# Layer norms of a two-block network: statistics gathered while the products before run, the norm's end on columns of 128 tokens, and constant products on TensorE around it

## The reference, abridged

```python
def layer_norm(x, g, b):
    mu = jnp.mean(x, -1); var = jnp.mean(jnp.square(x - mu), -1)
    return (x - mu) * lax.rsqrt(var + LN_EPS) * g + b
...
    for i in range(DEPTH):            # 2 layers: gated delta net, then short conv mixer
        h = layer_norm(ALPHA * h + mix, ...)                       # norms 0 and 2
        h = layer_norm(ALPHA * h + conv_ffn(h, ...), ...)          # norms 1 and 3
...
    x = x + 0.5 * g1 * swiglu(modulate(rms_norm(x, ...)), ...)     # norm 4
    x = x + g2 * mixer(modulate(rms_norm(x, ...)))                 # norm 5
    x = x + 0.5 * g3 * swiglu(modulate(rms_norm(x, ...)), ...)     # norm 6
    return rms_norm(x, final_norm)                                 # norm 7
```

## Time and profile before

| | us |
|---|---|
| median of 3 runs | 1393.05 (1392.62 to 1393.16) |
| the profiled execution's own time | 1394.26 |
| its span in the trace | 1392.6 |
| TensorE busy | 1309.7 (94%) |
| VectorE busy | 989.1 (71%) |
| ScalarE busy | 792.6 (57%) |

### The profile page before, as it was taken

One profiled execution on the slowest core, in us unless ns is written; L12 is line 12 of the kernel. 1 busy time (PEld: TensorE's weight loads), 2 busy tenths in 40 slices (PEclk: granted clock), 3 DMA queues, 4 the chain that ended last, 5 costly groups with the idle time before them and its releaser, 6 DMA issues.

```text
span 1392.6 us, 28808 instructions
## 1 busy us (share of the span) xinstructions
PE 1309.7 (94%) x10370; PEld 1280.7 (92%) x10370; DVE 989.1 (71%) x1727; ACT 792.6 (57%) x1165; POOL 45.2 (3%) x83
## 2 busy tenths in 40 slices
PE   6997999899999999999999889999899999999997
PEld 5996999789999889889999789999799988999996
DVE  7777653879897789779894577774556666777744
ACT  5868233477773354477773467763455554777632
POOL 0001000000001101000100000000000000000000
PEclk9989999999999999999999989999999999999998
DMA  6431002438788768648785435565445334465651
GB/s 234 148 110 60 1 32 76 167 121 275 273 305 292 257 200 282 227 140 289 275 296 183 130 92 188 186 210 184 155 137 167 122 107 136 150 198 181 217 179 42
DMA packets 65339, 244.44 MB, mean 176 GB/s; under 512 B 7264, under 2 KB 9600, under 8 KB 65280
## 3 DMA queue, kind: packets, MB, share of 16 engines
q1 hardware_dynamic: 54624, 204.70, 43.9%
q0 software_dynamic: 10656, 38.93, 8.5%
HBM read 242.56 MB, written 1.05 MB: 175 GB/s over the span
## 4 chain that ended last, share of the span: by engine, by line
PE 86%; DVE 7%; ACT 5%; issue 2%; DMA 0%; DVEq 0%; ACTq 0%; SPq 0%
PE ps L1375 23%; PE ps L1376 23%; PE ps L1377 23%; PE ps L1389 2%; PE ps L1507 2%; PE ps L1517 2%; DVE wlo L319 2%; PE ps L1390 1%; PE ps L1620 1%; DVE tb L863 1%; PE ps L1395 1%; ACT whi L312 1%; PE ps L1666 1%; PE ps L1455 1%; PE ps L1668 1%
## 5 line engine op out<-in xcount | busy, mean ns | idle before, releaser
L1375 PE MATMUL ps<-hhi,whi 128*128 128x258 f32 (+4 forms) x2064 | 591.6, 287 | 7.3 <-DVE ab L1243 2.7
L1376 PE MATMUL ps<-hlo,whi 128*128 128x258 f32 (+4 forms) x2064 | 587.7, 285 | 0.0
L1377 PE MATMUL ps<-hhi,wlo 128*128 128x258 f32 (+4 forms) x2064 | 586.8, 284 | 0.0
L312 ACT ACTIVATE whi<-raw 128x1024 fp32r<-128x1024 f32 (+1 forms) x360 | 399.9, 1112 | 284.5 <-PE ps L1377 261.6
L319 DVE TENSOR_TENSOR wlo<-raw,whi 128x1024 fp32r<-128x1024 f32 (+1 forms) x360 | 462.2, 1292 | 109.6 <-ACT whi L312 108.4
L1375 PEld LDWEIGHTS ps<-hhi,whi 128*128 128x128 f32 x2064 | 393.6, 191 | 8.6 <-issue 6.1
L1376 PEld LDWEIGHTS ps<-hlo,whi 128*128 128x128 f32 x2064 | 394.0, 191 | 0.5 <-issue 0.2
L1377 PEld LDWEIGHTS ps<-hhi,wlo 128*128 128x128 f32 x2064 | 394.4, 191 | 0.0
L1375 PE MATMUL ps<-ahi,whi 128*128 128x256 f32 (+2 forms) x768 | 216.0, 281 | 1.4 <-DVE alo L1156 1.4
L1376 PE MATMUL ps<-alo,whi 128*128 128x256 f32 (+2 forms) x768 | 216.3, 282 | 0.0
L1377 PE MATMUL ps<-ahi,wlo 128*128 128x256 f32 (+2 forms) x768 | 215.8, 281 | 0.0
(11 more groups left out here) (339 smaller groups left out, 1468.8 us busy)
## 6 DMA issues: line engine op xcount, KB each, us to landing
raw<-in_w_up SPq DMA_DIRECT2D x176, 512.0 KB, 3.5
raw<-in_w_down SPq DMA_DIRECT2D x64, 704.0 KB, 4.3
ring<-in_ada_w POOLq DMA_DIRECT2D x72, 512.0 KB, 4.5
raw<-in_w_mix SPq DMA_DIRECT2D x48, 512.0 KB, 3.4
raw<-in_w_a_in SPq DMA_DIRECT2D x32, 512.0 KB, 3.5
raw<-in_w_b_cx SPq DMA_DIRECT2D x16, 512.0 KB, 4.4
raw<-in_w_a_out SPq DMA_DIRECT2D x8, 512.0 KB, 3.5
raw<-in_w_b_gate SPq DMA_DIRECT2D x8, 512.0 KB, 4.4
```

What stands on the lines that cost most here:

```text
L312: nc.scalar.activation(whi[:, s, 0:blocks * P], raw[:, s, 0:blocks * P], ACT.Copy).then_inc(hi_split, 1)
L1375: nc.tensor.matmul(out, whi[:, s, w], rhi(k0 + k), start=first and k == 0, stop=False)
L1376: nc.tensor.matmul(out, whi[:, s, w], rlo(k0 + k), start=False, stop=False)
L1377: ins = nc.tensor.matmul(out, wlo[:, s, w], rhi(k0 + k), start=False, stop=last and k == blocks - 1)
```

## The change

- **Layer norms 0 to 3.** A provisional mean (`shift`) is taken from the first two tiles by one PE product in the middle of the phase (`shift_mm`). DVE subtracts it from the tiles already there, and from the residual before later tiles are added (`centre_residual`). ACT squares each tile during the phase (`act_before_ln`), DVE sums the squares (`square_up`). When the last tile comes, only its own sum and square are missing.
- **Columns.** PE multiplies data (as weights) by one column of `C_MEAN` (`columns`), so that the sums of 128 tokens stand as one column of 128 partitions. Variance, guess and Newton step run on 3 columns (2 where there are 256 tokens). `row` spreads a column back over all partitions by a transpose of a broadcast column. What is left of the mean (`rest`) is subtracted tile by tile (`take_rest`), for tiles 0 to 3 ahead of the gain products, for 4 to 7 between them.
- **Norms 5 and 7** get the same end; seven tiles' squares are reduced on PE before the last half unit (`seven_squares_mm`).
- **Constant products.** `keep_busy` issues 3 and then 4 fp32 products of constants (10 after norm 3, none in norm 7) around the last `row`.
- **first_step** runs tile by tile over three slots at once (two for `x`, `rms0`, `rms2`).
- The split of the last slot before the norm (`meanwhile`) moves from the middle of `dve_norm` to its end. The PE programs of `down0`, `down1`, `b_out` and `a_out` are written out instead of looped. ACT's 1/sqrt table is loaded ahead of the last tile, and the Silu table right after the guess, and the reloads inside the `up` loops are gone. POOL's first loads for `ada_w` wait until `a_out` is done. `spread` uses banks 1, 4, 5, 6, 0 so that bank 2 is free for the third slot. `down_squares` and `act_down_squares` are reordered around the last tile in the same manner.

```diff
-SUMS_AT = {i: i * KT for i in range(8)}
+SUMS_AT = {0: 0, 1: 7, 2: 14, 3: 21, 4: 28, 5: 36, 6: 43, 7: 51}
+LN_AHEAD = 4
+IDLE_PRODUCTS = {0: (3, 4), 1: (3, 4), 2: (3, 4), 3: (3, 10), 5: (3, 4), 7: (0, 0)}
+SC_REST, SC_REST2, SC_VAR, SC_GUESS, SC_TMP, SC_RSTD = range(320, 344, 4)
+RAW_TILES = {"a_out": 3, "down0": 2, "b_out": 3, "down1": 2}
+SHIFT_TILES = 2
...
+        def groups_of(n):
+return 2 if n == SEQ else 3
+        def group(n, j):
+o = j * P if (j + 1) * P <= n else n - P
+return slice(o, o + P)
...
+pool.wait_ge(tiles_read, SLOTS + PH["up0"].first)
...
+def act_before_ln(i, name, n):
+    phase = PH[name]
+    per = 2 if phase.blocks == SLOT_BLOCKS else 1
+    t0, k, after = phase.first // SLOTS, phase.units // SLOTS, BLOCKS_AFTER[name]
+    if name != "a_out":
+        mine(nc.scalar.activation(small[:, 314:315], eps_of(LN_EPS), ACT.Abs_reciprocal_sqrt))
+    def square(m):
+        act.wait_ge(xc_ready, i * KT + m + 1)
+        if m >= 2:
+            act.wait_ge(sq_sum, i * (KT - 1) + max(2, m - 1))
+        nc.scalar.activation(ab[:, m % 2, 0:n], xb[:, m, 0:n], ACT.Square).then_inc(sq_ready, 1)
+    done = 0
+    for u in range(phase.units):
+        if u == phase.units - 1:
+            square(KT - 1)
+        split_hi(act, t0 + u // SLOTS + 1, u % SLOTS, phase.blocks if u // SLOTS < k - 1 else after)
+        tiles = (u + 1) // per
+        if name == "a_out" and u == SLOTS:
+            act.wait_ge(ld_c, 16)
+            nc.scalar.activation(cb[:], cb[:], ACT.Silu).then_inc(c_ready, 1)
+            act.wait_ge(eps_ready, 1)
+            mine(nc.scalar.activation(small[:, 314:315], eps_of(LN_EPS), ACT.Abs_reciprocal_sqrt))
+        if u % per == per - 1 and tiles > RAW_TILES[name] and tiles < KT:
+            while done < tiles:
+                square(done)
+                done += 1
...
+    g = groups_of(n)
+    if i < 4:
+        act.wait_ge(v_ready, i + 1)
+        nc.scalar.activation(sc(SC_GUESS, g), sc(SC_VAR, g), ACT.Abs_reciprocal_sqrt).then_inc(guess_ready, 1)
+        if i in (0, 2):
+            mine(nc.scalar.activation(small[:, 312:313], eps_of(eps), ACT.Silu))
+    else:
+        act.wait_ge(var_mm, i + 1)
+        nc.scalar.activation(sc(SC_GUESS, g), ps[5][:, 0:g], ACT.Abs_reciprocal_sqrt, bias=eps_of(eps)).then_inc(guess_ready, 1)
...
+    mine(nc.scalar.activation(small[:, 312:313], eps_of(RMS_EPS), ACT.Silu))
...
+def dve_residual(norm, name, n, off):
...
+    t0, k, after, raw_tiles = phase.first // SLOTS, phase.units // SLOTS, BLOCKS_AFTER[name], RAW_TILES[name]
+    shift, squares = tb[:, 0, 0:n], sb[:, 0, 0:n]
+    x_of = lambda m: xb[:, m, 0:n]
+    h_of = lambda m: hf[:, m, off:off + n]
+    def lo_of(u):
+        split_lo(dve, t0 + u // SLOTS + 1, u % SLOTS, phase.blocks if u // SLOTS < k - 1 else after)
+    def sum_up(m):
+        if m == 0:
+            return
+        dve.wait_ge(tiles_read, SLOTS + phase.first + (m + 1) * per)
+        if m > 1:
+            dve.wait_ge(sum_ready, SUMS_AT[norm] + m)
+        nc.vector.tensor_tensor(sums[:, 0:n], x_of(0) if m == 1 else sums[:, 0:n], x_of(m), ALU.add).then_inc(sum_ready, 2 if m == 1 else 1)
+    def square_up(m):
+        dve.wait_ge(sq_ready, norm * KT + m + 1)
+        if m > 1:
+            dve.wait_ge(sq_sum, norm * (KT - 1) + m)
+        if m:
+            nc.vector.tensor_tensor(squares, ab[:, 0, 0:n] if m == 1 else squares, ab[:, m % 2, 0:n], ALU.add).then_inc(sq_sum, 2 if m == 1 else 1)
+    def centre_residual(m):
+        step(nc.vector.scalar_tensor_tensor(h_of(m), h_of(m), ALPHA, shift, ALU.mult, ALU.subtract))
+    squared = 0
+    for m in range(KT):
+        u = (m + 1) * per - 1
+        if m == KT - 1 and per == 2:
+            lo_of(u - 1)
+        dve.wait_ge(unit_done, phase.first + u + 1)
+        bank = ps[(u - per + 1) % SLOTS][:, 0:n]
+        if m < raw_tiles:
+            nc.vector.scalar_tensor_tensor(x_of(m), h_of(m), ALPHA, bank, ALU.mult, ALU.add).then_inc(tiles_read, per)
+            if m < SHIFT_TILES:
+                sum_up(m)
+        else:
+            nc.vector.tensor_tensor(x_of(m), h_of(m), bank, ALU.add).then_inc(xc_ready, 1)
+            if m == KT - 1:
+                break
+            nc.vector.memset(small[:, 310:311], 0.0).then_inc(tiles_read, per)
+            sum_up(m)
+            centre_residual(m + 1)
+        for j in range(u - per + 1, u + 1):
+            lo_of(j)
+            if per == 2 and j == u - 1:
+                while m > raw_tiles and squared < m:
+                    square_up(squared)
+                    squared += 1
+            if name in ADA_AT:
+                dve_ada(ADA_AT[name] + j, j % 2)
+        if m == raw_tiles - 1:
+            dve.wait_ge(mean_mm, 2 * norm + 1)
+            step(nc.vector.tensor_scalar(shift, ps[4][:, 0:n], KT / SHIFT_TILES, None, ALU.mult))
+            if m >= SHIFT_TILES:
+                sum_up(m)
+            for j in range(raw_tiles):
+                if j == raw_tiles - 1:
+                    dve.wait_ge(sum_ready, SUMS_AT[norm] + raw_tiles)
+                    step(nc.vector.scalar_tensor_tensor(sums[:, 0:n], shift, -float(raw_tiles), sums[:, 0:n], ALU.mult, ALU.add))
+                nc.vector.tensor_tensor(x_of(j), x_of(j), shift, ALU.subtract).then_inc(xc_ready, 1)
+            centre_residual(m + 1)
+        while m >= raw_tiles and squared <= m:
+            square_up(squared)
+            squared += 1
+    nc.vector.memset(small[:, 310:311], 0.0).then_inc(tiles_read, per)
+    return lambda: lo_of(phase.units - 1)
...
+    g = groups_of(n)
+    dst = xb if dst is None else dst
+    def take_rest(m):
+        mine(nc.vector.tensor_tensor(xb[:, m, 0:n], xb[:, m, 0:n], ps[6][:, 0:n], ALU.subtract))
...
+        dve.wait_ge(mean_mm, 2 * i + 2)
+        nc.vector.tensor_copy(sc(SC_REST, g), ps[4][:, 0:g]).then_inc(rest_col, 1)
+        dve.wait_ge(rest_col, i + 1)
+        step(nc.vector.tensor_tensor(sc(SC_REST2, g), sc(SC_REST, g), sc(SC_REST, g), ALU.mult))
+        dve.wait_ge(var_mm, i + 1)
+        nc.vector.scalar_tensor_tensor(sc(SC_VAR, g), ps[5][:, 0:g], eps, sc(SC_REST2, g), ALU.add, ALU.subtract).then_inc(v_ready, 1)
+        dve.wait_ge(rest_row, i + 1)
+        take_rest(0)
...
+    step(nc.vector.tensor_tensor(sc(SC_TMP, g), sc(SC_GUESS, g), sc(SC_GUESS, g), ALU.mult))
+    if i < 4:
+        step(nc.vector.tensor_tensor(sc(SC_TMP, g), sc(SC_VAR, g), sc(SC_TMP, g), ALU.mult))
+    else:
+        step(nc.vector.scalar_tensor_tensor(sc(SC_TMP, g), ps[5][:, 0:g], eps, sc(SC_TMP, g), ALU.add, ALU.mult))
+    nc.vector.scalar_tensor_tensor(sc(SC_RSTD, g), sc(SC_TMP, g), 3.0, sc(SC_GUESS, g), ALU.subtract, ALU.mult).then_inc(rstd_col, 1)
+    if i < 4:
+        for m in range(1, LN_AHEAD):
+            take_rest(m)
+    dve.wait_ge(rstd_row, {0: 1, 1: 2, 2: 3, 3: 4, 5: 5, 7: 6}[i])
+    y_ = ps[7][:, 0:n]
...
+        if i < 4 and m >= LN_AHEAD:
+            take_rest(m)
+        if i < 4:
+            mine.after()
...
+    if meanwhile:
+        meanwhile()
...
-def first_step(t, n, version, norm=None):
-    for s in range(2):
+def first_step(t, n, version, norm=None, until=SLOTS):
+    ahead = 3 if version in ("gdn", "ln0", "ln1", "ln2", "rms1") else 2
+    for s in range(ahead):
         pe.wait_ge(lo_split, t * SLOTS + s + 1)
         pe.wait_ge(tiles_read, t * SLOTS + s + 1)
-        for k in range(KT):
-            if s == 0:
-                pe.wait_ge(rhs_hi, RHS_AT[version] + k + 1)
-            w = slice(k * P, (k + 1) * P)
+    for k in range(KT):
+        pe.wait_ge(rhs_hi, RHS_AT[version] + k + 1)
+        w = slice(k * P, (k + 1) * P)
+        for s in range(ahead):
             nc.tensor.matmul(ps[s][:, 0:n], whi[:, s, w], hhi[:, k, 0:n], start=k == 0, stop=False)
             nc.tensor.matmul(ps[s][:, 0:n], wlo[:, s, w], hhi[:, k, 0:n], start=False, stop=False)
-    for s in range(2):
+    for s in range(ahead):
         for k in range(KT):
             if s == 0:
                 pe.wait_ge(rhs_ready, RHS_AT[version] + k + 1)
             ins = nc.tensor.matmul(ps[s][:, 0:n], whi[:, s, k * P:(k + 1) * P], hlo[:, k, 0:n], start=False, stop=k == KT - 1)
         ins.then_inc(unit_done, 1)
-    for s in range(2, SLOTS):
+    for s in range(ahead, until):
...
+    def half(t, s, also=None):
+        h0 = SLOT_BLOCKS * (s % 2)
+        unit(t, s, SLOT_BLOCKS, n, lambda k: ahi[:, k, 0:n], lambda k: alo[:, k, 0:n], out=ps[s - s % 2][:, 0:n],
+             first=s % 2 == 0, last=s % 2 == 1, k0=h0,
+             k_wait=also or (wait_for(h0, range(FT)) if s < 2 else None))
+    if norm in (5, 7):
+        t1 = t0 + PH[name].units // SLOTS - 1
+        with pe.Fori(t0, t1) as t:
+            for s in range(SLOTS):
+                half(t, s)
...
+            if s == SLOTS - 1:
+                seven_squares_mm(norm, n)
+            half(t1, s)
+        pe_norm(norm, n)
+        return
+    for u in range(PH[name].units):
```

(50 more changed lines are left out.)

156 lines of the change are left out of this document (60 added, 96 removed).

## The result

The changed kernel takes 1383.8 us (median of 6 runs, 1379.1 to 1387.4) against 1393.1 for the kernel before on the same chip (1390.8 to 1396.1): ratio 0.9926, 95% interval 0.9904 to 0.9948. The forecast was 1378.8, faster. The profiled execution has a span of 1380.1 us, 12.5 less than before, where 14.2 were forecast.

A forecast was written before the change was run, and what follows sets the result against it. TensorE, busy 94% of a 1392.6 us span, bounds the kernel, so only its starvation around norms can be won. The terms sum to -14.2 us: span 1378.4, median 1378.8; own bounds 1371 to 1387, with most of two rivals 1367.5 to 1389.

The forecast's parts named there:

- Chain, 4.9 us: Last tile's read to first gain product: 4.9 us instead of 11.4 in norm 0, 3.6 in norm 5.
- 1.3 for the low clock in norms 0 and 2: Added to the chains of norms 0 and 2, the clock being down after TensorE's wait: +1.3 us each.
- First step, 14.0 us behind the first gain product: First gain product to fourth unit's end: 14.0 us, between 13.4 and 14.6; before 15.3; norm 5 reckoned with 14.6.
- What the order is worth, 1.3 us: The first step in norm 0, with products now tile by tile: -1.3 us.
- Squares' wait 3.1 us in `b_out`, 17.7 us behind unit 2: In `b_out` the seventh square is summed 17.7 us after unit 2, TensorE wants it at 14.6: 3.1 us standing.
- Norm 1, 0.3 us for the two operations behind the last split: Within norm 1's 20.4 us, two `ada` operations now behind the last split: 0.3 us.
- Norm 3, -1.8: Norm 3 with the late norm 4: -1.8 us, between -0.8 and -2.9; first product of `up2` at 802.8 instead of 803.65.
- `a_in`, nothing: The phase `a_in`: no change forecast, 0 us.
- End of the kernel, and norm 6: End of the kernel, small Newton step and no table load in the chain: -0.7 us; norm 6: -1.2 us.
- Clock held, VectorE keeps up: Rival, chance 0.22: clock stays up and VectorE keeps pace in `a_out` and `b_out`; 11 us more won, 1367.5.
- Constants do not hold the clock: Rival, chance 0.14: first steps run 3.4 us more at half rate, VectorE falls further behind; +10 us, 1389.
- Straight-line code: Rival, slower than before, chance 0.04: over 0.0105 us per unlooped product loses all; at 15% the time is 1403.

The follow-up runs named there:

- e5: The changed kernel with 12 more constant products in each of `a_out` and `b_out`, ahead of the wait for the summed squares: 1380.3 us.
- e1: The changed kernel without its constant products in all five norms: 1387.5 us.
- e2: The changed kernel with the first step's products in the old order, two units ahead and unit by unit: 1390.6 us.
- e4: The changed kernel with the additions of squared tiles in `a_out` and `b_out` on GpSimd instead of VectorE: 1376.0 us.
- e7: e4 plus `a_in`'s first step in the old order and `a_out`'s first two weight splits behind the sum of tiles 0 and 1: 1374.4 us.
- e8: e7 with e6's moves, and the two `ada` operations behind norm 1 moved into `down1`: 1368.6 us.
- e3: The changed kernel with `a_in`'s first step in the old order and the two `ada` operations behind norm 1 moved to the end of `b_cx`: 1383.9 us.
- e10: The changed kernel itself, run again: 1381.8 us.
- e6: The changed kernel with norm 3's last weight split behind its square additions and norm 4's statistics behind `up2`'s second unit: 1379.1 us.

## Why the prediction was right, point by point

- **What bounds.** Right: apart from `a_in` and low stretches of the clock, only TensorE's standing around the norms moved.
- **Chain, 4.9 us and 1.3 for the low clock in norms 0 and 2.** Measured 6.4 in both (6.2 forecast), 5.3 in norm 1, 3.1 in norm 5 (3.6 forecast). The close sum is in part luck: at full clock the chain takes 4.4 (e5), 0.5 less than reckoned, and the low clock costs 1.4 to 2.0 instead of 1.3. The reason given, that TensorE stands before the last tile, is shown for norms 0 and 2 by e5, and it is not the whole: norm 1 has no such wait, was given no term for the clock, and its chain ran at 0.60.
- **First step, 14.0 us behind the first gain product.** Measured 13.6, 13.7 and 13.5. The forecast left the clock open between 13.4 and 14.6; the constants lifted it (e1). In norm 5, where the forecast took 14.6, it was up throughout and the step took 12.7: with the shorter chain 5.8 us won instead of 3.4 (5.3 after what `down2` pays), the largest term that was mis-sized. Of it, e1 puts 1.6 us down to the constants.
- **What the order is worth, 1.3 us.** Too low in e2: 2.1 and 2.0 us at the fourth units of norms 0 and 2 (the clock apart), 1.2 and 1.0 in norms 5 and 6, though 0.9 at the end of `b_cx`.
- **Squares' wait 3.1 us in `b_out`, 17.7 us behind unit 2.** Measured 3.23 and 17.65, and none in `down0`. In `a_out` 3.87. Its cause, VectorE's queue, is shown by e4. The phases lost 4.7 (4.4 forecast) and 4.4 (3.4 forecast). The 1.0 more in `a_out` is the low clock on its last three products, which was priced in the chain alone: from the end of the wait to the end of the phase are 2.3 us, and 1.3 in e5. The wait for the mean product, 1.4 us, is not in the sum either, but e7 shows that it is no loss of its own.
- **Norm 1, 0.3 us for the two operations behind the last split.** Measured 1.2: the first step came out shorter than reckoned, and so VectorE, 2.4 us behind, showed. e8 takes it away.
- **Norm 3, -1.8.** Measured -1.5, with the first product of `up2` 12.3 us behind `down1` (12.4 forecast); the clock fell in spite of ten constants.
- **`a_in`, nothing.** This is the step that failed outright: the diff's `first_step` serves version `"x"` too, and now waits for two units' weights before the first product, 1.2 us, confirmed by e3. The forecast looked at that function only behind norms. The other 1.5 us of the 2.8 are low stretches of the clock and not the order: from the first product to the end of `a_in` are 225.8 us before, in e2, e3 and e4, 227.3 here, 227.1 in e10 and up to 229.0 in e6. The 1.3 won in `mix` do not repeat in e10.
- **End of the kernel, and norm 6.** -1.2 for the end proper, less 0.4 in `down3`, and -1.1: as forecast. In e10 a low stretch of the clock at 1180.8 takes the gain of norm 6 away again (15.5 us from `mix` to the fourth unit, 15.1 before, 14.0 in the first profile).
- **Rivals.** "Clock held, VectorE keeps up" was right in its first half for the first steps and wrong in its second. Its terms add up to 11.1 us, so 1367.7 and not 1367.5. "Constants do not hold the clock" fell in e1. The forecast's sign of being too slow, a clock of 1.00 through a norm, came up in norm 5. Straight-line code costs nothing that shows: `down0`, now without a loop, takes 64.4 us instead of 63.3, and its mean product and columns were forecast at 1.2.

Of the 5 us between 1378.8 and 1383.8, 1.7 are the sum's (a span of 1380.1 instead of 1378.4). That the sum came so close is partly luck: 2.8 us too much in `a_in`, 1.2 in norm 1 and 0.8 in norm 0 stand against norm 5, 1.9 us shorter than forecast, and the rest of `mix`, 1.3 shorter. The other 3.3 lie between span and median: 3.7 us in this set, 0.2 in that of e10, where the forecast took the 0.45 of the kernel before. That is the spread of executions, and the granted clock goes with it: of the six, the fastest has a span of 1377.4 at a mean clock of 0.978, the slowest 1385.7 at 0.969. Which of the low stretches decide it was not tried.

## What to carry to other kernels

When statistics move from behind a phase into it, the queue of the engine that gathers them decides: count its work per tile against the consumer's pace, and find where the last partial sum stands in that queue. Ask of every function in a diff who else calls it. Put spare work where its engine waits for others anyway: the same two operations cost 3.9 us ahead of `b_gate` and nothing in `down1`. And test each part by itself: the change is named after its statistics, but e2 puts most of its gain down to the order of the first step.

## What the runs showed of the hardware

- The clock decides over short products as well: three one-column products in fp32 take 0.7 to 0.8 us at full clock (e5, norm 2) and 1.3 to 1.4 at half (the changed kernel, norm 0); three constant products 0.83 and 1.49.
- With constant products in the chain the first steps behind norms 0, 1 and 2 ran at 0.94 to 1.00, without them at 0.79 to 0.84. In norm 3, where 5.3 us of standing follow them, the clock was down at the first product with them as well.
- The clock also fell in the chain of norm 1, ahead of which TensorE had no wait for squares: 0.60 over the 6.6 us behind `down0` in the changed kernel, 0.78 over 5.6 us in e10, 1.00 over 5.6 us in e5.
- An addition of 258 columns takes GpSimd 0.73 to 0.97 us alone (e4; two close together 2.43) where VectorE takes 0.42, and an overlapping split on VectorE lasts 1.65 us instead of 1.22.
